# Head lengths of the delta rule from high and low parts of the squares, and one tap of the convolution on ScalarE

## What is computed

```python
proj = h @ w_in[l]
gq, gk, gv, gz, ga, gb, sq, sk, sv = jnp.split(proj, split_points, axis=-1)
qkv = jax.nn.silu(causal_depthwise_conv(jnp.concatenate([gq, gk, gv], axis=-1), conv_w[l]))
gq, gk, gv = jnp.split(qkv, 3, axis=-1)
q_g = l2_norm(heads(gq))      # x * rsqrt(sum(x * x over the 64 channels of a head) + 1e-6)
k_g = l2_norm(heads(gk))
```

## Time and profile before

| | us |
|---|---|
| median of 3 runs (1248.77 to 1250.81) | 1250.73 |
| the profiled execution | 1250.88 |
| its span in the trace | 1248.8 |
| TensorE matmul busy | 1222.2 (98%) |
| TensorE weight load busy | 996.5 (80%) |
| VectorE busy | 704.9 (56%) |
| ScalarE busy | 489.1 (39%) |
| GpSimd busy | 107.6 (9%) |
| mean granted TensorE clock, share of full | 0.996 |

### The profile page before, as it was taken

One profiled execution on the slowest core, in us unless ns is written; L12 is line 12 of the kernel. 1 busy time (PEld: TensorE's weight loads), 2 busy tenths in 40 slices (PEclk: granted clock), 3 DMA queues, 4 the chain that ended last, 5 costly groups with the idle time before them and its releaser, 6 DMA issues.

```text
span 1248.8 us, 19942 instructions
## 1 busy us (share of the span) xinstructions
PE 1222.2 (98%) x8398; PEld 996.5 (80%) x8398; DVE 704.9 (56%) x1035; ACT 489.1 (39%) x768; POOL 107.6 (9%) x152
## 2 busy tenths in 40 slices
PE   6999999998999999999999999999999999999998
PEld 3767878778888888888888889898776778888886
DVE  5699978655476553323333567767666555343344
ACT  4343643664246222112222344214475662322232
POOL 4000005611030000000000110000012210000000
PEclk9899999999999999999999999999999999999999
DMA  9557711003023542333322342334123025333301
GB/s 339 211 164 223 253 40 37 3 4 104 2 76 116 179 141 77 94 116 112 101 77 62 99 136 78 102 93 83 49 68 79 3 73 138 90 89 98 113 34 68
DMA packets 149927, 125.58 MB, mean 101 GB/s; under 512 B 15952, under 2 KB 133489, under 8 KB 149712
## 3 DMA queue, kind: packets, MB, share of 16 engines
q1 hardware_dynamic: 148416, 121.98, 32.3%
q0 software_dynamic: 1232, 2.07, 0.5%
q10 hardware_dynamic: 192, 0.27, 0.1%
HBM read 122.20 MB, written 2.10 MB: 100 GB/s over the span
## 4 chain that ended last, share of the span: by engine, by line
PE 91%; DVE 4%; ACT 2%; issue 1%; DMA 1%; DVEq 0%; POOL 0%; SPq 0%; ACTq 0%
PE bank L605 53%; PE bank L876 6%; PE bank L698 4%; PE bank L1344 4%; PE bank L1314 4%; PE bank L1378 3%; PE bank L1233 2%; PE bank L734 1%; PE bank L1065 1%; PE bank L649 1%; DMA hscratch<-in_w_ada_dram 1%; PE bank L1269 1%; PE bank L1286 1%; PE bank L825 1%; PE bank L1246 1%
## 5 line engine op out<-in xcount | busy, mean ns | idle before, releaser
L605 PE MATMUL bank<-hsplit,whi 128*128 128x512 f32 (+1 forms) x1840 | 542.5, 379 | 1.5 <-DVE wlo L2128 1.4
L605 PEld LDWEIGHTS bank<-hsplit,whi 128*128 128x128 f32 x1840 | 334.9, 188 | 73.6 <-issue 10.0
L605 PE MATMUL bank<-hsplit,wlo 128*128 128x512 f32 (+1 forms) x920 | 346.0, 376 | 0.0
L2128 DVE TENSOR_TENSOR wlo<-ring,whi 128x2048 fp32r<-128x2048 f32 (+4 forms) x100 | 200.4, 2005 | 176.6 <-ACT whi L1583 176.3
L1583 ACT ACTIVATE whi<-ring 128x2048 fp32r<-128x2048 f32 (+4 forms) x100 | 168.5, 1685 | 124.2 <-DVE xT L2527 53.3
L605 PEld LDWEIGHTS bank<-hsplit,wlo 128*128 128x128 f32 x920 | 172.9, 188 | 32.3
L605 PE MATMUL bank<-a_split,whi 128*128 128x512 f32 x340 | 104.7, 389 | 0.0
L605 PEld LDWEIGHTS bank<-a_split,whi 128*128 128x128 f32 x340 | 63.8, 188 | 13.3
L605 PE MATMUL bank<-a_split,wlo 128*128 128x512 f32 x170 | 66.1, 389 | 0.0
L1526 POOL TENSOR_TENSOR acc<-acc,tb 128x512 f32<-128x512 f32 x12 | 17.8, 1480 | 424.7 <-ACT tb L1841 424.7
L1587 ACT ACTIVATE a_split<-tb 128x512 fp32r<-128x512 f32 x22 | 13.8, 633 | 88.1 <-DVE tb L2577 87.9
(11 more groups left out here) (477 smaller groups left out, 1794.9 us busy)
## 6 DMA issues: line engine op xcount, KB each, us to landing
ring<-in_w_in_dram SPq DMA_DIRECT2D x22, 1024.0 KB, 5.3
ring<-in_w_in_dram SPq DMA_DIRECT2D x34, 512.0 KB, 5.0
ring<-in_w_ada_dram SPq DMA_DIRECT2D x16, 1024.0 KB, 5.1
ring<-in_w_gate_dram SPq DMA_DIRECT2D x11, 1024.0 KB, 5.4
ring<-in_w_up_dram SPq DMA_DIRECT2D x11, 1024.0 KB, 5.4
ring<-in_w_down_dram SPq DMA_DIRECT2D x8, 768.0 KB, 4.7
ring<-in_w_down_dram SPq DMA_DIRECT2D x8, 640.0 KB, 4.2
hscratch<-in_w_ada_dram SPq DMA_DIRECT2D x4, 1024.0 KB, 14.8
```

Of the source, the lines that this page charges most:

```text
L605: last = mm(o[0:m, 0:n], w[:, k, c0:c0 + m], rhs(s, k), start=k + i == 0, stop=k == kn - 1 and i == 2)
L2128: split_lo = splitter(dve, None, lambda lo, src, hi: tt(lo, src, hi, ALU.subtract))
```

## The change

1. Head lengths: ScalarE copies `pick` to type fp32r once. Behind the square of a chunk it makes the high part of the squares (`hsq_hi`), VectorE makes the low part (`length_lo`, `hsq_lo`), and TensorE does two fp32r matmuls in place of one fp32 matmul. Both parts have three buffers. TensorE's length m now waits for VectorE's low part, and stands behind the projection of chunk m + 5 (before: m + 4); the last stands behind `ab`.
2. Convolution: ScalarE forms tap 3 straight out of PSUM, by a second copy with the tap as scale, and VectorE adds the three others: one instruction less for each of the 12 chunks. VectorE waits for the second copy.
3. The buffer waits of ScalarE follow: `raw` is free after the third tap, the buffer of squares after the low part, the buffer of high parts after TensorE's step three before. The wait for the constants moves up to m = 3.

```diff
--- before.py
+++ after.py
@@ -237,6 +237,8 @@
         gates = A1.take(2 * T)
         glog, grow = gates[:, 0:T], gates[:, T:2 * T]
         hsq = [tb[i][:, 0:T] for i in range(2)]
+        hsq_split = arena_r[:, 12 * T:18 * T].rearrange("p (s b t) -> p s b t", s=2, b=3)
+        pick_r = arena_r[:, 18 * T:18 * T + CONST_W["pick"][1]]
         sacc = acc_buf[:, 0:T]
         row_buf = [A1.take(T) for _ in range(2)]
         base1 = A1.at
@@ -706,16 +708,18 @@
             def h_ready(tag):
                 return lambda k: done("h" + tag, k)
 
-            pick = cst("pick").rearrange("p (w j c) -> p w j c", w=2, j=NJ)
+            pick = pick_r.rearrange("p (w j c) -> p w j c", w=2, j=NJ)
             length_tile = [None]
 
             def head_lengths(m):
 
                 if m == 0:
                     length_tile[0] = open_tile(pe, "hsum", hold=True)
-                    pe.wait_ge(*arrived("const_rest"))
-                pe.wait_ge(*done("hsq", m))
-                last = mm(length_tile[0][0:40, :], pick[:, m // 4, m % 4, :], hsq[m % 2], start=m == 0, stop=m == 7)
+                    pe.wait_ge(*done("act_vectors", "pick"))
+                pe.wait_ge(*done("dve_vectors", "hsq_lo", m))
+                for s in range(2):
+                    last = mm(length_tile[0][0:40, :], pick[:, m // 4, m % 4, :], hsq_split[:, s, m % 3, :],
+                              start=m + s == 0, stop=m + s == 8)
                 last.then_inc(*(fill("hsum") if m == 7 else signal("hsum_step", m)))
                 if m == 7:
                     let_go("hsum")
@@ -754,11 +758,12 @@
                     meta_columns()
                 elif m >= 4:
                     project(("pj", m), f"qkv{m // 2}", P * (m % 2), P, hx, T, release=m % 2 == 1)
-                if m >= 4:
-                    head_lengths(m - 4)
+                if m >= 5:
+                    head_lengths(m - 5)
                 if m >= 7 and m % 2 == 1:
                     ada((m - 7) // 2 + 4)
             project(("ab",), "abk", 0, P, hx, T)
+            head_lengths(7)
             project(("sk",), "abk", 40, P, hx, T, release=True)
             project(("sv",), "sv", 0, P, hx, T, release=True)
 
@@ -1632,19 +1637,24 @@
             def conv_in(m):
                 act.wait_ge(*filled("pj", m))
                 if m >= 3:
-                    act.wait_ge(*done("conv", m - 3, 3))
-                A(raw[m % 3][:, 3:], bank("pj", m)[:, :], ACT.Copy).then_inc(*read("pj", m))
+                    act.wait_ge(*done("conv", m - 3, 2))
+                A(raw[m % 3][:, 3:], bank("pj", m)[:, :], ACT.Copy)
+                A(qkv[:, m, :], bank("pj", m)[:, :], ACT.Copy, scale=V2[:, 36 + m:37 + m]).then_inc(*read("pj", m))
 
             def conv_out(m):
-                act.wait_ge(*done("conv", m, 3))
+                act.wait_ge(*done("conv", m, 2))
                 A(qkv[:, m, :], qkv[:, m, :], ACT.Silu).then_inc(*signal("silu", m))
 
             act.wait_ge(*done("rawpad"))
             def head_square(m):
                 if m >= 2:
-                    act.wait_ge(*done("hsum_step", m - 2))
+                    act.wait_ge(*done("dve_vectors", "hsq_lo", m - 2))
                 act.wait_ge(*done("silu", m))
                 A(hsq[m % 2], qkv[:, m, :], ACT.Square).then_inc(*signal("hsq", m))
+                if m >= 3:
+                    act.wait_ge(*done("hsum_step", m - 3))
+                act.wait_ge(*done("hsq", m))
+                A(hsq_split[:, 0, m % 3, :], hsq[m % 2], ACT.Copy).then_inc(*signal("act_vectors", "hsq_hi", m))
 
             for m in range(14):
                 if m < 12:
@@ -1656,9 +1666,11 @@
                         split_hi()
                 if m >= 2:
                     conv_out(m - 2)
+                if m == 3:
+                    act.wait_ge(*arrived("const_rest"))
+                    A(pick_r, cst("pick"), ACT.Copy).then_inc(*signal("act_vectors", "pick"))
                 if 3 <= m < 11:
                     head_square(m - 3)
-            act.wait_ge(*arrived("const_rest"))
             for r0 in (0, HD):
                 A(sel_r[r0:r0 + 40, :], cst("sel", 40), ACT.Copy).then_inc(*signal("sel_r"))
             act.wait_ge(*filled("ab"))
@@ -2273,14 +2285,24 @@
             def conv4(m):
                 dve.wait_ge(*copied("pj", m))
                 tap = lambda k: V2[:, 12 * k + m:12 * k + m + 1]
-                ts(qkv[:, m, :], raw[m % 3][:, 0:T], tap(0), None, ALU.mult).then_inc(*signal("conv", m, 0))
-                for k in range(1, 4):
-                    dve.wait_ge(*done("conv", m, k - 1))
+                for k in range(3):
+                    if k:
+                        dve.wait_ge(*done("conv", m, k - 1))
                     stt(out=qkv[:, m, :], in0=raw[m % 3][:, k:k + T], scalar=tap(k), in1=qkv[:, m, :],
                         op0=ALU.mult, op1=ALU.add).then_inc(*signal("conv", m, k))
 
+            def length_lo(m):
+
+                if m >= 3:
+                    dve.wait_ge(*done("hsum_step", m - 3))
+                dve.wait_ge(*done("act_vectors", "hsq_hi", m))
+                tt(hsq_split[:, 1, m % 3, :], hsq[m % 2], hsq_split[:, 0, m % 3, :].bitcast(F32), ALU.subtract)\
+                    .then_inc(*signal("dve_vectors", "hsq_lo", m))
+
             for m in range(12):
                 conv4(m)
+                if m >= 4:
+                    length_lo(m - 4)
                 if m == 1:
                     meta_scaled()
                 if m in SPLIT_AT:
```

## The result

The changed kernel took 1254.93 us (median of 6 runs, 1254.62 to 1258.89), the kernel before 1248.98 in the same comparison (6 runs, 1248.69 to 1250.81): a ratio of 1.0048, 95% interval 1.0038 to 1.0058. It is 5.9 us slower, which is more than 0.2%. Ratios are taken from fast runs: one run of a variant further down (pool_lo, 1517.49 us, still counted in its median of 1250.3, which is 1250.04 without it) and one of the kernel before beside it (2390.27) were slow ones. The profiled execution of the changed kernel took 1254.73 us.

A forecast was written before the change was run, and what follows sets the result against it. TensorE and VectorE were both taken to run at their limit in the stretch. Waits 6.7 + 2.2, clock 2.75, less savings 4.2 and 0.34, gave +7.1 on 1250.88, less 0.1: 1257.9 us, range 1255.2 to 1259.8.

The forecast's parts named there:

- The wait at the first length: TensorE at length 0 waits 6.7 us for VectorE's low part, which stands behind `ada_sum(4)` and chunk 4's taps.
- The later lengths: With the low clock, TensorE waits 2.2 us for VectorE at length 4; lengths 2, 6 and 7 wait for nothing.
- the other branch of the forecast: At full clock, TensorE waits 1.5, 0.7 and 0.8 us at lengths 2, 4 and 6.
- ScalarE at nothing: ScalarE's added taps, high parts and `pick` copy, some 14 us, fall in its idle time and cost nothing.
- What TensorE saves: Two fp32r passes take 0.46 us for 0.98: 0.52 per length, 4.2 over eight, 4.5 with the old 0.34 wait.
- The 0.32 stays: The 0.32 us on TensorE before each length stays, as a semaphore stands ahead of it in both kernels.
- The clock: TensorE's clock falls to half in the first wait and stays low 5.5 us after it: 2.75 us lost.
- the full clock: Rival, chance 0.13: TensorE's clock stays up; waits less savings give +5.2 us, 1256.0.
- the free lengths: Rival, chance 0.04: low parts are there when TensorE reaches the lengths, no waits; -4.5 us, 1246.3.
- unshortened passes: Rival, chance 0.04: a pair of passes still costs 0.98 us, with the same waits; about +10.3, 1261.1.
- The delay is made good later: Rival, chance 0.03: the stage behind 138 us is bound by VectorE alone and hides TensorE's loss; 1250.9.
- the last of the sum: Whole kernel: the +7.1 us is added to the profiled execution of 1250.88, less 0.1 towards the median: 1257.9.

The follow-up runs named there:

- pool_lo: The changed kernel with the low parts of the squares made by GpSimd instead of VectorE: 1250.3 us, ratio 1.001.
- ada_later: The changed kernel with each `ada_sum` block of VectorE moved one chunk later: 1248.75 us, ratio 0.9994; in a second comparison 1249.37, 1.0001.
- fill: The changed kernel with 27 short matmuls, result unread, ahead of the first length's wait: 1255.09 us, ratio 1.0048; a second time 1256.25.
- tap_only: The kernel before with only tap 3 moved to ScalarE and its buffer waits, lengths still one fp32 pass: 1250.41 us, ratio 1.0011.
- after_again: The changed kernel unaltered, run and profiled a second time: 1254.04 us, ratio 1.0037 to the kernel before.

## Why the prediction was right and where it was wrong

- **The wait at the first length**: foreseen 6.7 from VectorE's arrival, the low part done at 83.3; measured 6.74, low part done at 81.3. Everything ran 1.9 us earlier, 1.7 of them by estimate because the clock at 44 us had been low for half as long. Right, and ada_later shows that the order of VectorE's list makes it.
- **The later lengths**: a wait of 2.2 at length 4 and none at 2, 6 and 7; measured 2.43 and none. VectorE's first idle time was foreseen behind 97.0 and began at 95.1, which the earlier start of 1.9 explains. At full clock the other branch of the forecast (1.5, 0.7, 0.8) came in fill as 1.76, 0.90, 0.63. Right.
- **ScalarE at nothing**: right for the changed kernel; tap_only shows a wait of 1.49 us as soon as length 0 stands at its old place.
- **What TensorE saves** was mis-sized: "0.46 for two" is 0.47, but "The 0.32 stays" failed. Ahead of a pair the gap is 0.23 (88.96 to 89.19), and the first projections behind it no longer take 0.73 but 0.62 per two. That is 0.70 a length where nothing else stands between, 5.4 in all for 4.2.
- **The clock**: the forecast had one fall, 2.75 lost. The second profile has that (2.8); the first has two falls, 3.5 lost. The second wait was foreseen, but the step did not ask whether the clock falls there as well, and the runs show that it can and need not. In the first profile the two errors (-1.2 and +0.75), with the 0.2 more at length 4, nearly cancel, which is luck: 6.9 for 7.1. In the second, without the extra fall, it is 6.2.
- **The rivals**: the full clock did not come, nor the free lengths, nor unshortened passes. (The last was priced at +10.3; with "the same waits" and the 4.2 back it adds up to 7.1 + 4.2 = 11.3.) "The delay is made good later" is false as a mechanism, though "I find no slack that gives anything back" was too strict: 0.36 us came back behind 204.
- **The step that failed** is the last of the sum: "The profiled execution took 1250.88 [...] Forecast: 1250.88 + 7.1 - 0.1". The forecast is 3.0 us too high. Of these, 1.8 is the base: 1250.78 where six runs give a median of 1248.98. The profiled run had the longer low clock of rows 6, as only five of 17 profiles have, and the changed kernel was then put on top of it. The other 1.15 is the change itself, 7.1 for 5.95; the term behind that is the saving, 4.2 for 5.4, through "The 0.32 stays". On the later base the same 7.1 give 1256.1, inside the range. The range had room for the terms and none for the base, though three runs from 1248.77 to 1250.81 already showed 2 us of it.

The measured difference is 5.95; the stretch alone is 6.88 in one profile and 6.24 in the other. With the 0.36 that comes back behind 204 us these are 6.5 and 5.9. What is left is within the scatter of the clock at 44 us and of the waits without a releaser, and the runs don't divide it further.

## What to carry to other kernels

When an operand of TensorE moves to another engine, it arrives when that engine's list gets there: walk that list beside TensorE's, count what stands ahead of the operand, and compare the length of both lists over a whole period, because a block that is only moved turns up at a later wait. Waits in dense matmuls can cost clock on top: here 3.5 or 2.8 us, from one profile to the next, for 9.2 waited in two places, and nothing for 5.4 in four. Before an effect below 0.5% is added to a profiled run, look whether that run's own clock falls are a fixed part of it.

## What the runs showed of the hardware

- An elementwise instruction of GpSimd beside VectorE is not free: 36 taps of VectorE took 858 ns in the mean with eight of them in the stretch, 750 without, single ones 1.77 us for 0.75, and a tensor_scalar with one tile as input 1.43 for 0.48.
- Between an fp32r and an fp32 matmul 0.32 us passed, between two fp32r matmuls of different shape 0.23; the first two projections behind the fp32 matmul took 0.11 longer.
- The granted clock fell behind an idle time of only 1.76 us with one-column matmuls after it, in one profile of two of the same kernel, once behind 1.17 us (309.6 us), and did not fall behind 2.50 us in after_again. Its low stretches had 3.4, 6.8 and about 10 us, and one kernel had different ones at the same place from run to run.
